# Down projections of two expert groups moved ahead of the expert selection, with gating a group later, one-hot matrices built on VectorE alone, and low weight parts written in place

## The chip, the cores and the metric

The program runs on one NeuronCore of a Trainium2 chip. Its engines are TensorE (PE in the profile, with its weight loads as PEld), VectorE (DVE), ScalarE (ACT), GpSimd (POOL) and SyncE (SP, which here only issues transfers). They run side by side and order themselves by semaphores. The metric is the device time of one execution in microseconds (us), as the median of several runs.

## The reference

Two transformer blocks in float32 are applied to 256 tokens of width 2048. The part that the change rearranges is the mixture of experts at the end of the first block ("peer"): each token has 8 heads, each head picks 16 of 128 x 128 = 16384 experts, and every picked expert is one row of `w_down` and one row of `w_up`.

```python
q = einsum(xn, w_query); s = einsum(q, sub_keys)            # 8 heads, 2 halves, 128 keys
top_s, top_i = lax.top_k(s, 16)
cand = top_s[..., 0, :, None] + top_s[..., 1, None, :]       # 16 x 16 sums
cand_s, cand_i = lax.top_k(cand.reshape(..., 256), 16)
expert = i1 * 128 + i2
gates = softmax(cand_s)
a = gelu(einsum('cd,ced->ce', xc, w_down[expert])) * gates
out = einsum('ce,ced->cd', a, w_up[expert])
```

Around it stand an attention with a pooling branch before, and in the second block a differential and a latent attention with a gated feed-forward layer.

## The kernel before

**Dense experts.** The kernel does not gather rows. It multiplies all 16384 rows of `w_down` with the tokens, applies gelu, multiplies with a gate matrix G (expert x token, zero where the token did not pick the expert), and multiplies the result with all rows of `w_up`. The work is cut into 8 groups of 2048 experts. A group is 32 weight tiles of 1 MB (128 partitions x 2048 columns): 16 down tiles and 16 up tiles. So the stage has 256 tiles.

**Split precision.** A weight tile is used in four pieces of 512 columns. For each piece ScalarE copies the weights to a rounded high part (`high`, the activation in line 518), VectorE subtracts it from the weights to get the low part (`low`, line 1250), and TensorE forms three products for each of the four 128-column blocks of the piece (`piece`, lines 875 to 877): high x high, high x low and low x high. That is 48 matmuls of 256 columns a tile. `w_parts` holds the parts of four pieces, high beside low, so ScalarE and VectorE can be at most one tile ahead.

**The ring.** SyncE loads weight tiles into a ring of 4 slots. A slot is loaded again when VectorE has made the last low part from it (`split=` in `load`, a wait on `lo_ready`).

**Selection and gate matrix.** After the query projection (stage `wq`, 16 tiles) VectorE picks the best 16 of each half (`best`), then for two halves of the tokens (`tb`) the best 16 of the 256 sums, and turns them into indices and gates (lines 1427 to 1456). Then, in 64 steps of 4 tokens, it builds two one-hot matrices: `oh2` (line 1468) and `oh1` (line 1469), each 128 x 4 x 128. GpSimd multiplies `oh2` with the gates (line 490), and TensorE multiplies the two (line 1045), which gives the 128 x 128 gate matrix of one token. ScalarE copies it out and stores it to a scratch tensor in HBM (line 664). While this goes on, no weight tile is multiplied.

**The peer loop.** In each of the 8 turns of the loop VectorE makes the low parts of the next tile, then handles one tile: for a down tile `gated` (lines 1478, 1481, 1482: times G, high part, low part), for an up tile `expert_out` (line 1488: adds to the residual `hT`). The gating of a down tile follows on that tile's own gelu. In every second tile VectorE also reduces one row block of the second block's modulation matrix (`ada`, 12 a turn, lines 1508 and 1511), and 4 of them a second time with another vector (1508, written to PSUM). GpSimd loads these into two buffers, and one transfer of 2 MB a turn brings G of the group.

The order of the work on each engine is written out by hand; every engine runs its own list in order.

Of the kernel before, what the change touches and what calls it, by code (L numbers as in the profile page):

```python
# [13 lines left out]
P = 128  # L14
T = 256
# [34 lines left out]
OHT, OHB = 4, 4  # L50
TWO = 2
# [35 lines left out]
for _name, _n in (("mask0", 3 * P), ("mask1", 3 * T), ("cos1", T), ("sin1", T), ("perm1", P),  # L87
                  ("ident", P), ("cos2", T), ("sin2", T), ("perm2", P), ("iota", P), ("rcount", 4 * T), ("ones", P)):
    CONST[_name] = (_t, _t + _n)
    _t += _n  # L90
# [60 lines left out]
def build_program(nc, A, out):  # L151
    with ExitStack() as ctx:
# [13 lines left out]
        modt = sb("modt", [P, 16])  # L166
# [9 lines left out]
        assert nc.lookup_mloc("cb").addr == arena_at + 121 * 1024  # L176

# [45 lines left out]
        W1 = split_room("w_parts_1", 84, PIECES, 2, PB * P)  # L223

        GH, GL = split_room("merged_high", 0, KC, T), split_room("merged_low", 16, KC, T)
        WO = split_room("w_parts_out", 32, PIECES, 2, PB * P)
# [6 lines left out]
        oh1 = [room(56 + 4 * j, OHT, P) for j in range(OHB)]  # L233
        oh2 = [room(58 + 4 * j, OHT, P) for j in range(OHB)]
        stage = [room(72 + 8 * j, P, BLK) for j in range(2)]
        topv = room(72, 2 * KC, TOPK)
        topi = room(74, 2 * KC, TOPK, dt=U32)
        topf = room(90, KC, TOPK)
        cv = room(91, EH, TOPK)
        ci = room(91.5, EH, TOPK, dt=U32)  # L240
        ca = room(92, EH, TOPK, dt=U32)
        cbi = room(92.5, EH, TOPK, dt=U32)
        caf = room(93, EH, TOPK)
        cbf = room(93.5, EH, TOPK)
        ids = room(94, 3, EH * TOPK)
        idT = room(96, 3, T)
        gsum = room(99, EH)
# [3 lines left out]
        WP = split_room("w_parts", 80, PIECES, 2, PB * P)  # L251
        junk = ps[:, 4:8, :].rearrange("p a b -> p (a b)")
        gl = room(99.5, 2, T)
# [4 lines left out]
        W2 = split_room("w_parts_2", 113, PIECES, 2, PB * P)  # L258
# [19 lines left out]
        WO2 = split_room("w_parts_out_2", 0, PIECES, 2, PB * P)  # L278

        HH, HL = split_room("hidden_high", 32, FF, T), split_room("hidden_low", 92, FF, T)  # L280
        WF = split_room("w_parts_ff", 76, PIECES, 2, PB * P)
# [76 lines left out]
        oh_pool = sem("oh_pool")  # L358
# [5 lines left out]
        at_ready = sem("at_ready")  # L364
        lam_exp = sem("lam_exp")
# [22 lines left out]
        def _(sp):  # L388
            def load(slot, src, made, n=D, split=None):
# [8 lines left out]
            def stream(name, src, count, n=D, o_name=None):  # L398

                o = OUTS[o_name or name]  # L400
                with sp.Fori(0, count // U) as i:
                    for u in range(U):
                        load(u, src[i * U + u], i * U + (o + u + 1 - RING), n)
# [1428 lines left out]
```

## Time and profile before

| | us |
|---|---|
| median of 3 runs | 4149.68 |
| fastest and slowest run | 4144.1, 4150.41 |
| profiled execution, first to last instruction (its span) | 4145.4 |
| PE busy | 3714.2 (90%) |
| PEld busy | 3546.5 (86%) |
| DVE busy | 2687.2 (65%) |
| ACT busy | 1669.0 (40%) |
| POOL busy | 174.1 (4%) |
| mean granted TensorE clock | 0.957 of full speed |

The span is taken inside one profiled execution; the median of the runs is 4.3 us above it, which is what lies around the first and the last instruction. Busy shares are means over stages that differ much: in one stretch of some 220 us before the peer loop TensorE has little to do, and VectorE has almost no idle time. A busy PE is not a PE at its peak, since matmuls are pipelined: in the peer loop one matmul is shown with 0.28 us and they start every 0.12 us.

### The profile page before, as it was taken

The numbers are of one execution on the slowest core, as the hardware profiler recorded it, in microseconds if no ns is written. First come the engines' busy times: TensorE is split into PE (matmuls) and PEld (weight loads), VectorE is DVE, ScalarE is ACT, GpSimd is POOL, SyncE is SP. The second block draws the span as 40 slices with busy tenths as digits, with TensorE's granted clock in tenths as the row PEclk, the third lists the DMA queues.
The fourth block names the chain that finished last, engine by engine and source line by source line (L and its number), as shares of the span: only waits on it lengthen the run. The fifth ranks groups of instructions, "written<-read, shape, count | busy, mean of one in ns | idle before, by whom it ended". The sixth has DMA issues, their size and how long they took to land.

```text
span 4145.4 us, 73928 instructions
## 1 busy us (share of the span) xinstructions
PE 3714.2 (90%) x27694; PEld 3546.5 (86%) x27694; DVE 2687.2 (65%) x4416; ACT 1669.0 (40%) x2865; POOL 174.1 (4%) x240
## 2 busy tenths in 40 slices
PE   0888999891789999999999999979988989999998
PEld 0887888891689999999999999968955989999997
DVE  7865433579967768777777777662237566666554
ACT  0532211440244444444444444442226455555443
POOL 0000000001600000000000000000000000000000
PEclk8999999995899999999999999989999999999999
DMA  9875774440367576766767676622220435555453
GB/s 412 323 263 194 273 288 148 152 163 20 132 244 285 212 287 225 273 240 260 254 255 252 249 282 223 256 92 92 93 80 1 151 134 182 182 182 181 161 178 129
DMA packets 129661, 829.37 MB, mean 200 GB/s; under 512 B 12784, under 2 KB 29296, under 8 KB 38256
## 3 DMA queue, kind: packets, MB, share of 16 engines
q1 hardware_dynamic: 87984, 619.20, 40.7%
q0 software_dynamic: 24768, 189.80, 12.4%
q10 hardware_dynamic: 16640, 16.78, 1.2%
q8 instruction: 168, 2.75, 0.3%
q14 instruction: 101, 0.83, 0.1%
HBM read 806.86 MB, written 18.87 MB: 199 GB/s over the span
## 4 chain that ended last, share of the span: by engine, by line
PE 81%; DVE 10%; issue 4%; DMA 2%; ACT 2%; DVEq 0%; SPq 0%; POOL 0%; ACTq 0%; POOLq 0%
PE ps L875 22%; PE ps L877 21%; PE ps L876 21%; PE ps L851 8%; DMA arena<-in_ada 2%; PE ps L907 1%; PE ps L909 1%; PE ps L910 1%; PE ps L845 1%; DVE arena L1468 1%; DVE w_parts L1250 1%; DVE arena L1469 1%; ACT w_parts L518 1%; PE ps L1152 1%; ACT arena L518 0%
## 5 line engine op out<-in xcount | busy, mean ns | idle before, releaser
L518 ACT ACTIVATE w_parts<-ring 128x512 fp32r<-128x512 f32 x1352 | 851.5, 632 | 1185.9 <-PE ps L877 1042.4
L1250 DVE TENSOR_TENSOR w_parts<-ring,w_parts 128x512 fp32r<-128x512 f32 x1352 | 899.1, 690 | 639.5 <-ACT w_parts L518 617.7
L875 PE MATMUL ps<-x_high,w_parts 128*128 128x256 f32 (+1 forms) x3040 | 892.7, 294 | 135.4 <-DVE w_parts L1250 116.4
L876 PE MATMUL ps<-x_low,w_parts 128*128 128x256 f32 (+1 forms) x3040 | 884.0, 291 | 0.0
L877 PE MATMUL ps<-x_high,w_parts 128*128 128x256 f32 (+1 forms) x3040 | 883.5, 291 | 0.0
L875 PEld LDWEIGHTS ps<-x_high,w_parts 128*128 128x128 f32 x3040 | 587.8, 193 | 155.1 <-DVE w_parts L1250 111.2
L876 PEld LDWEIGHTS ps<-x_low,w_parts 128*128 128x128 f32 x3040 | 588.1, 193 | 6.7
L877 PEld LDWEIGHTS ps<-x_high,w_parts 128*128 128x128 f32 x3040 | 587.7, 193 | 6.9
L875 PE MATMUL ps<-at_high,w_parts 128*128 128x256 f32 x2048 | 580.4, 283 | 0.0
L876 PE MATMUL ps<-at_low,w_parts 128*128 128x256 f32 x2048 | 579.5, 283 | 0.0
L877 PE MATMUL ps<-at_high,w_parts 128*128 128x256 f32 x2048 | 579.5, 283 | 0.0
L1250 DVE TENSOR_TENSOR w_parts_ff<-ring,w_parts_ff 128x512 fp32r<-128x512 f32 (+1 forms) x544 | 363.1, 676 | 245.8 <-ACT w_parts_ff L518 239.2
L518 ACT ACTIVATE w_parts_ff<-ring 128x512 fp32r<-128x512 f32 (+1 forms) x544 | 336.3, 619 | 384.7 <-PE ps L877 384.5
L875 PE MATMUL ps<-x_high,w_parts_ff 128*128 128x256 f32 x1408 | 399.6, 284 | 17.1 <-DVE w_parts_ff L1250 17.1
L876 PE MATMUL ps<-x_low,w_parts_ff 128*128 128x256 f32 x1408 | 399.4, 284 | 0.0
L877 PE MATMUL ps<-x_high,w_parts_ff 128*128 128x256 f32 x1408 | 399.3, 284 | 0.0
L875 PEld LDWEIGHTS ps<-at_high,w_parts 128*128 128x128 f32 x2048 | 393.1, 192 | 0.9
L876 PEld LDWEIGHTS ps<-at_low,w_parts 128*128 128x128 f32 x2048 | 393.2, 192 | 0.0
L877 PEld LDWEIGHTS ps<-at_high,w_parts 128*128 128x128 f32 x2048 | 393.1, 192 | 0.0
L851 PE MATMUL ps<-arena,ring 128*128 128x256 f32 (+1 forms) x1536 | 344.6, 385 | 1.9 <-DVE arena L1226 1.3
L851 PEld LDWEIGHTS ps<-arena,ring 128*128 128x128 f32 x1536 | 290.7, 190 | 49.1 <-issue 8.5
L518 ACT ACTIVATE arena<-ps 128x256 f32<-128x256 f32 (+3 forms) x350 | 154.5, 444 | 412.8 <-PE ps L851 245.7
(212 smaller groups left out, 5899.0 us busy)
## 6 DMA issues: line engine op xcount, KB each, us to landing
ada<-in_ada POOLq DMA_DIRECT2D x160, 1024.0 KB, 5.1
ring<-in_peer_down SPq DMA_DIRECT2D x128, 1024.0 KB, 5.2
ring<-in_peer_up SPq DMA_DIRECT2D x128, 1024.0 KB, 5.0
ring<-in_w_in SPq DMA_DIRECT2D x102, 1024.0 KB, 4.8
ring<-in_w_up SPq DMA_DIRECT2D x88, 1024.0 KB, 4.8
ring<-in_w_down SPq DMA_DIRECT2D x64, 704.0 KB, 4.0
arena<-in_ada SPq DMA_DIRECT2D x32, 1024.0 KB, 19.5
ring<-in_w_out SPq DMA_DIRECT2D x16, 1024.0 KB, 4.8
```

Source lines behind the costliest of these rows:

```text
L518: return nc.scalar.activation(*a, **k)
L845: ins = mm(ps[:, 4, 0:cols], ones, sqd[:, k, :], start=(k == 0), stop=(k == n - 1))
L851: ins = mm(to, ring[:, slot % RING, (at + k) * P:(at + k + 1) * P], moving(k), start=(k == 0), stop=(k == n - 1))
L875: mm(to, w_high, high(k), start=(k == 0), stop=False)
L876: mm(to, w_high, low(k), start=False, stop=False)
L877: ins = mm(to, w_low, high(k), start=False, stop=(k == k_all - 1))
L907: mm(to, high[:, k, tok], w_high, start=(k == 0 and tb % 2 == 0), stop=False, skip_group_check=True)
L909: mm(to, low[:, k, tok], w_high, start=False, stop=False, skip_group_check=True)
L910: ins = mm(to, high[:, k, tok], w_low, start=False, stop=(k == KC - 1), skip_group_check=True)
L1152: ins = mm(ps[:, 7, (u % 2) * P:(u % 2 + 1) * P], vv[:, kb, h * P:(h + 1) * P], wt2[u % 2][:, kb * P:(kb + 1) * P], start=(kb == 0), stop= ...
L1250: vv.tensor_tensor(parts[:, m, 1, 0:w], ring[:, slot, j * PB * P:j * PB * P + w], parts[:, m, 0, 0:w].bitcast(F32), ALU.subtract).then_inc ...
L1468: vv.tensor_tensor(oh2[j], many, idT[:, 1, tok].unsqueeze(2).broadcast_to([P, OHT, P]), ALU.is_equal)
```

## The change

**What moves.** The 32 down tiles of groups 0 and 1 are multiplied before and during the selection and the building of the gate matrix. Their gelu results are kept in two buffers (`held`), which lie in the room of the old `ada` buffers and at the end of the arena. From then on the order of tiles is up(g), down(g + 2), and the gating of group g + 1 runs on VectorE beside the down tiles of group g + 2, from `held`. The PE loop over 8 turns of 32 tiles becomes 32 tiles, a loop of 3 turns of 64 tiles, and 32 tiles. The selection is cut into 12 parts (`choose`), each behind the low parts of one tile.

**One-hots.** The matrices are built on VectorE alone with `tensor_scalar` instructions of 128 x 128: three a token, 12 a step. The first compares with one pointer scalar, the second and the third compare and multiply with the high and the low part of the gate (two pointer scalars). GpSimd's multiplication is gone. TensorE multiplies the rounded type, two matmuls a token. A step stands behind each piece of the tiles 16 to 28, and a fifth behind each tile.

**Low parts in the ring.** VectorE writes the low part over the weights in the ring (`ring_low`), `w_parts` holds high parts alone, and a ring slot is loaded again when TensorE has used the tile (`acc_full`), in the last stage when it has used the pieces.

**Modulation rows.** The 96 row blocks are read in the 3 turns (30 a turn) and the last 32 tiles (6), through one buffer `ada2`. Of three blocks in a row the first is reduced twice: in an odd tile with the context vector, in the next tile with the other, and only then is the buffer free.

VectorE in the loop before, up tiles (line 1488 `expert_out`, line 1511 a modulation row, line 1250 low parts; `ISA` is the reduction, its second row reads the sum):

```order
L1488 SCALAR_TENSOR_TENSOR hT<-ps,mod,hT 128x256
L1511 ISA ada,modt<-ada,cb 128x2048
L1511 ISA modt 128x1
L1249 REGISTER_ALU
L1250 TENSOR_TENSOR w_parts<-ring,w_parts 128x512
L1249 REGISTER_ALU
L1250 TENSOR_TENSOR w_parts<-ring,w_parts 128x512
L1249 REGISTER_ALU
L1250 TENSOR_TENSOR w_parts<-ring,w_parts 128x512
L1249 REGISTER_ALU
L1250 TENSOR_TENSOR w_parts<-ring,w_parts 128x512
L1487 REGISTER_ALU
```

Here one reduction stands behind `expert_out`, and the tile after it has none.

VectorE in the loop now, in the second tile of a turn (line 1620 `expert_out`, 1656 the wait for the load, 1627 the reduction with the context vector):

```order
L1620 SCALAR_TENSOR_TENSOR hT<-ps,mod,hT 128x256
L1656 ISA
L1627 ISA ps,modt<-const,cb 128x2048
L1627 ISA modt 128x1
L137 ISA
```

Four low parts and the next tile's `expert_out` follow. The same list one tile further (1624 the reduction with the other vector, behind which the buffer is free):

```order
L1335 TENSOR_TENSOR ring_low<-ring,w_parts 128x512
L1619 REGISTER_ALU
L1620 SCALAR_TENSOR_TENSOR hT<-ps,mod,hT 128x256
L1624 ISA const,modt<-const,cb 128x2048
L1624 ISA modt 128x1
L1334 REGISTER_ALU
L1335 TENSOR_TENSOR ring_low<-ring,w_parts 128x512
```

Now two of them follow in neighbouring tiles, and a third, which needs a newly loaded buffer, in the tile after.

VectorE behind the selection before (line 1456 the last of the gates, 1468 and 1469 the one-hots of one step):

```order
L1455 RECIPROCAL arena<-arena 128x8
L1456 TENSOR_TENSOR arena<-arena 128x128
L1462 UNCONDITIONAL_BRANCH
L1462 ISA
L1468 ISA
L1468 TENSOR_TENSOR arena<-const,arena 128x512
L1469 ISA
L1469 TENSOR_TENSOR arena<-const,arena 128x512
L1466 REGISTER_ALU
```

VectorE at that place now (line 1580 the last of the gates, 1631 the low part of the gates, 1602 to 1604 the three one-hots of one token; three more tokens of the step follow before the next row of line 1335):

```order
L1579 RECIPROCAL const<-const 128x8
L1580 TENSOR_TENSOR const<-const 128x128
L1335 TENSOR_TENSOR ring_low<-ring,w_parts 128x512 x4
L1631 TENSOR_TENSOR const<-const 128x256
L1602 TENSOR_SCALAR one_hots<-const 128x128
L1603 TENSOR_SCALAR one_hots<-const 128x128
L1604 TENSOR_SCALAR one_hots<-const 128x128
L1602 TENSOR_SCALAR one_hots<-const 128x128
```

Two instructions a step became twelve, and low parts of weight tiles stand between the steps.

TensorE there now (lines 919 to 921 the three products of a down tile, 1095 and 1096 the high and low gates of a token):

```order
L920 MATMUL ps<-x_low,w_parts 128x256
L921 MATMUL ps<-x_high,ring_low 128x256
L1095 MATMUL ps<-one_hots 128x128
L1096 MATMUL ps<-one_hots 128x128
L1095 MATMUL ps<-one_hots 128x128
L1096 MATMUL ps<-one_hots 128x128
L1095 MATMUL ps<-one_hots 128x128
L1096 MATMUL ps<-one_hots 128x128
L1095 MATMUL ps<-one_hots 128x128
L1096 MATMUL ps<-one_hots 128x128
L919 MATMUL ps<-x_high,w_parts 128x256
```

Before, only the gate matmuls stood there, four a step. The core of the diff:

```diff
+        ring_low = nc.alloc_sbuf_tensor_at("ring_low", [P, RING, D], F32R, offset=nc.lookup_mloc("ring").addr)[:]
-        WP = split_room("w_parts", 80, PIECES, 2, PB * P)
+        WP = split_room("w_parts", 80, PIECES, PB * P)
+        hots = split_room("one_hots", 32, OHB, 3, OHT, P)
+        ada2 = spare(0, D)
+        held = [ada[:, :, :].rearrange("p a b -> p (a b)").rearrange("p (a b) -> p a b", a=16), room(88, 16, T)]
...
@@ SyncE @@
-                if split is not None:
-                    sp.wait_ge(lo_ready, split)
...
-                        load(t, src[t], None, split=16 + SPLIT[name] + PIECES * (t + 1 - RING))
+                        load(t, src[t], OUTS[name] + t + 1 - RING)
...
@@ GpSimd @@
-                    nc.gpsimd.tensor_tensor(
-                        oh2[j], oh2[j], idT[:, 2, tok].unsqueeze(2).broadcast_to([P, OHT, P]), ALU.mult,
-                    ).then_inc(oh_pool, 1)
...
+            gates_in(0, 0, 0)
+            gates_in(0, 0, 1)
+            with pool_e.Fori(0, 3) as i:
+                for r in range(ADA_ALL):
+                    pool_e.wait_ge(a2_free, i * ADA_ALL + (r + 1))
+                    pool_e.dma_start(ada2, A["ada"][i * ADA_ALL + (97 + r)]).then_inc(a2_in, 16)
+                    if r in (14, 29):
+                        gates_in(i, 32, 2 + r // 15)
...
@@ TensorE @@
-                    w_high, w_low = (parts[:, m, h, b * P:(b + 1) * P] for h in range(2))
+                    w_high = parts[:, m, b * P:(b + 1) * P]
+                    w_low = ring_low[:, slot, (at + b) * P:(at + b + 1) * P]
...
+            for s in range(32):
...
+                for j in range(PIECES):
+                    peer_piece(0, 0, s, s, j, XH, XL)
+                    if s == 16 and j == 0:
+                        pe.wait_ge(ids_copied, 2)
+                    if s >= 16 and 5 * (s - 16) + j < STEPS:
+                        gates_of(5 * (s - 16) + j)
...
+                if s in (10, 15):
+                    turn_ids((s - 10) // 5)
...
@@ VectorE @@
+            def hot_step(n):
+                dve.wait_ge(g_full, n + 1)
+                for q in range(OHT):
+                    t = OHT * n + q
+                    one_hot = hots[:, n % OHB, :, q, :]
+                    id1, id2 = idT[:, 0, t:t + 1], idT[:, 1, t:t + 1]
+                    vv.tensor_scalar(one_hot[:, 0, :], iota, id1, None, ALU.is_equal)
+                    vv.tensor_scalar(one_hot[:, 1, :], iota, id2, gate_h[:, t:t + 1], ALU.is_equal, ALU.mult)
+                    ins = vv.tensor_scalar(one_hot[:, 2, :], iota, id2, gate_l[:, t:t + 1], ALU.is_equal, ALU.mult)
+                ins.then_inc(oh_dve, 1)
...
+            for s in range(16):
+                peer_low(0, 0, s)
+                if s < 4:
+                    heads_best(12 + s)
+                else:
+                    choose((s - 4) // 6, (s - 4) % 6)
...
+            for s in range(16, 31):
+                for j in range(PIECES):
+                    if 5 * (s - 16) + j < STEPS:
+                        hot_step(5 * (s - 16) + j)
+                    low_piece(WP, SPLIT["peer"] + PIECES * (s + 1) + 1, s + 1, (s + 1) % RING, j)
+                if 5 * (s - 16) + 4 < STEPS:
+                    hot_step(5 * (s - 16) + 4)
+            for u in range(16):
+                gated(0, 0, 0, u, ATH, ATL)
+                if u % 4 == 3:
+                    low_piece(WP, SPLIT["peer"] + PIECES * 32 + 1, 32, 0, u // 4)
...
+            with dve.Fori(0, 3) as i:
+                for v in range(64):
+                    peer_low(i, 64, 33 + v)
+                    if v % 32 < 16:
+                        expert_out(i, 64, v % 16, 32 + v)
+                    else:
+                        gated(i, 32, 1 + v // 32, v % 16, ATH, ATL)
+                    r = (v - 1) // 2
+                    if v % 2 and r < ADA_ALL:
+                        dve.wait_ge(a2_in, i * (16 * ADA_ALL) + 16 * (r + 1))
+                        if r % 3 == 0:
+                            ada_ctx(modt[:, 30 + r // 3:31 + r // 3])
+                        else:
+                            ada_x(modt[:, ADA_X + r - r // 3 - 1:ADA_X + r - r // 3])
+                    if v % 2 == 0 and v and r % 3 == 0 and r < ADA_ALL:
+                        ada_x(modt[:, r // 3:r // 3 + 1])
```

## Rows read from the trace of the kernel before

**Rows 1.** The page's first line.

```profile
span 4145.4 us, 73928 instructions
```

**Rows 2.** Stretches: length, PE, PEld, DVE, ACT, POOL busy, PEclk, DMA share, GB/s.

```profile
932.00:1010.00 78.00, 1.80 (x6) 1.00 (x6) 74.47 (x206) 3.38 (x6) 0.00 (x0) 0.51 0.00 0
1010.00:1120.00 110.00, 78.05 (x424) 66.82 (x424) 110.00 (x110) 31.16 (x53) 69.50 (x54) 0.82 0.34 116
```

**Rows 3.** Timeline of ScalarE: start, length, instruction, idle before and its releaser.

```profile
930.27 0.38 ACT L518 ACTIVATE arena<-ps 128x256 f32<-128x256 f32 x1 [5.15 <-PE ps L877]
```

**Rows 4.** Timeline of TensorE in the peer loop.

```profile
1156.23 0.58 PE L875 MATMUL ps<-x_high,w_parts 128*128 128x256 f32 x1 [14.13 <-DVE w_parts L1250]
...
1349.83 0.58 PE L875 MATMUL ps<-x_high,w_parts 128*128 128x256 f32 x1 [2.92 <-issue]
...
1411.66 0.39 PE L875 MATMUL ps<-x_high,w_parts 128*128 128x256 f32 x1 [0.26 <-DVE w_parts L1250]
...
1541.93 0.38 PE L875 MATMUL ps<-x_high,w_parts 128*128 128x256 f32 x1 [2.56 <-DVE hT L1488]
```

**Rows 5.** The chain of waits: start, length, what, between 800 and 980.

```profile
822.52 6.42 DVE x_low L1264 x16
...
940.24 2.21 DVE cb L1430
...
974.03 2.21 DVE cb L1430
```

**Rows 6.** Timeline of VectorE around the selection's end.

```profile
957.83 0.23 DVE L1433 TENSOR_SCALAR arena<-arena 128x128 uint32<-128x128 uint32 x1
957.98 0.22 DVE L1434 TENSOR_SCALAR arena<-arena 128x128 uint32<-128x128 uint32 x1
...
1007.20 0.29 DVE L1456 TENSOR_TENSOR arena<-arena 128x128 f32<-128x128 f32 x1
1009.40 0.69 DVE L1468 TENSOR_TENSOR arena<-const,arena 128x512 f32<-128x512 f32 x1 [1.91 <-ACT arena L518]
```

**Rows 7.** Groups of VectorE, 750 to 1130: count, busy us, mean ns, idle before.

```profile
L1469 DVE TENSOR_TENSOR arena<-const,arena 128x512 f32<-128x512 f32 x60 | 90.5, 1509 | 0.0
...
L1264 DVE SCALAR_TENSOR_TENSOR x_low<-arena,mod,x_high 128x256 fp32r<-128x256 f32 x16 | 6.4, 480 | 0.0
```

**Rows 8.** Groups of VectorE, whole span: two pointer scalars, then one.

```profile
L1576 DVE TENSOR_SCALAR ada<-ada,small 128x512 f32<-128x512 f32 x16 | 8.7, 546 | 0.6
L1582 DVE TENSOR_SCALAR ada<-ada,small 128x512 f32<-128x512 f32 x16 | 7.8, 486 | 0.6
```

**Rows 9.** Timeline of VectorE in the peer loop: a down tile, then an up tile.

```profile
1395.27 0.42 DVE L1478 TENSOR_TENSOR arena<-arena 128x256 f32<-128x256 f32 x1
...
1396.66 2.29 DVE L1511 CUSTOM_DVE_ANT_0 ada<-ada,cb 128x2048 f32<-128x2048 f32 x1 [0.19 <-DVE at_low L1482]
...
1454.68 2.29 DVE L1511 CUSTOM_DVE_ANT_0 ada<-ada,cb 128x2048 f32<-128x2048 f32 x1
...
1456.88 1.90 DVE L1250 TENSOR_TENSOR w_parts<-ring,w_parts 128x512 fp32r<-128x512 f32 x3
1459.43 0.69 DVE L1250 TENSOR_TENSOR w_parts<-ring,w_parts 128x512 fp32r<-128x512 f32 x1 [0.66 <-ACT w_parts L518]
```

**Rows 10.** Timeline of GpSimd beside those up tiles.

```profile
1457.62 0.53 POOL L476 DMA_DIRECT2D ada<-in_ada  x1 [10.14 <-DVE modt L1511]
1469.14 0.53 POOL L476 DMA_DIRECT2D ada<-in_ada  x1 [10.99 <-DVE modt L1511]
```

**Rows 11.** Timeline of GpSimd: a load of 1 MB is issued.

```profile
397.12 0.53 POOL L476 DMA_DIRECT2D ada<-in_ada  x1 [8.16 <-DVE mod L1210]
```

**Rows 12.** Timeline of VectorE: the reduction that waited for that load.

```profile
402.21 2.29 DVE L1210 CUSTOM_DVE_ANT_0 ada<-ada,cb 128x2048 f32<-128x2048 f32 x1 [3.53 <-DMA ada<-in_ada]
```

**Rows 13.** Transfers issued from 1130 to 1160: count, KB, median us to landing.

```profile
gates_scratch<-arena ACTq DMA_DIRECT2D x2, 1024.0 KB, 7.6
arena<-gates_scratch POOLq DMA_DIRECT2D x1, 2048.0 KB, 8.2
```

More of the change, by code:

```diff
@@ L388, in _, with load @@
         def _(sp):
-            def load(slot, src, made, n=D, split=None):
+            def load(slot, src, made, n=D):
                 if made is not None:
                     sp.wait_ge(acc_full, made)
-                if split is not None:
-                    sp.wait_ge(lo_ready, split)
                 sp.dma_start(ring[:, slot % RING, 0:n], src).then_inc(w_slot[slot % RING], 16)
[L398 to L403, printed above, removed]
             sp.dma_start(cb[:, 0, :], A["c"]).then_inc(c_in, 16)
@@ L656, in _ @@
[L656 to L665 removed]
+                cols = slice(tb * P, (tb + 1) * P)
@@ L867, in tokens_first, with piece @@
                 return ins
-            def piece(to, parts, m, wait, first, n, high, low, k_all):
+            def piece(to, parts, m, wait, slot, at, first, n, high, low, k_all):
                 pe.wait_ge(lo_ready, wait)
@@ L1028, in _, with peer_piece, turn_ids @@
                     keys_of(n // 2 - 1)
-            keys_of(EH - 1)
-            for tb in range(2):
+            def peer_piece(i, per, at, u, j, high, low):
+                ins = piece(ps[:, u % BANKS, 0:T], WP, j, i * (per * PIECES) + (16 + SPLIT["peer"] + PIECES * at + j + 1),
+                            u % RING, PB * j, PB * j, PB, lambda k: high[:, k, :], lambda k: low[:, k, :], KC)
+                ins.then_inc(piece_used if j < PIECES - 1 else acc_full, 1)
+            def turn_ids(tb):
                 pe.wait_ge(ids_ready, tb + 1)
@@ new lines, in up_tile @@
+            def up_tile(i, per, g, u, at, high, low):
+                if u < BANKS and g < 7:
+                    pe.wait_ge(gelu_done, i * (per // 2) + (16 * (g + 2) - BANKS + u + 1) if g < 6 else 125 + u)
+                else:
+                    pe.wait_ge(up_free, i * (per // 2) + (16 * g + u - BANKS + 1))
+                for j in range(PIECES):
+                    if u == 0:
+                        pe.wait_ge(at_ready, i * (per // 2) + (16 * g + PB * (j + 1)))
+                    peer_piece(i, per, at, u, j, high, low)
@@ new lines, in _ @@
+            ch.leave(3)
+            dve.wait_ge(acc_full, OUTS["peer"] + 224)
+            for v in range(32):
+                if v < 31:
+                    peer_low(0, 0, 225 + v)
+                expert_out(0, 0, v % 16, 224 + v)
+                if v < 16:
+                    gated(0, 0, 7, v, XH, XL)
+                r = v // 2 - 8
+                if v % 2 and 0 <= r < 6:
+                    dve.wait_ge(a2_in, 16 * (3 * ADA_ALL + r + 1))
+                    if r % 3 == 0:
+                        ada_ctx(modc[:, 30 + r // 3:31 + r // 3])
+                        ada_x(mod2[:, 30 + r // 3:31 + r // 3])
+                    else:
+                        ada_x(mod2[:, 92 + r - r // 3 - 1:93 + r - r // 3 - 1])
```

494 lines of the change are left out of this document (276 added, 218 removed).

## The prediction, made before the change was run

> **What bounds the kernel now.** I read the stretches first, to see which engine fills each stage, then the chain of waits, then the timelines of the engines in turn. The profiled execution spans 4145.4 us [rows 1]; the median of the runs is 4149.7, so 4.3 us are added at the end. Two places matter.
>
> The first is the selection. The last tile of the query projection is copied out at 930.27 [rows 3], so TensorE ends it at 930.1, and the first tile of the peer loop starts at 1156.23 [rows 4]. Between them VectorE works without a break: 74.5 of 78 us in the selection and 110 of 110 while the one-hots are built [rows 2]. VectorE is the bound for 226 us, with TensorE all but idle in the first part.
>
> The second is the peer loop. GpSimd's loads follow VectorE's reductions in every second tile, 11.52 us apart [rows 10], so an undisturbed tile takes 5.76 us: TensorE is the bound there. A turn of 32 tiles takes 1541.93 - 1349.83 = 192.1 us [rows 4] where 32 x 5.76 is 184.3. The other 7.8 us are the branch back (2.9 [rows 4], "issue") and small waits for low parts such as the 0.26 of [rows 4].
>
> **The change part by part.** I follow the engines from 930.1 until tile 32 (the first up tile) is done. Before, tile 32 is the first of the second turn, done at 1349.8 + 5.9 = 1355.7.
>
> *Four tiles under the last of the first selection.* They run at TensorE's pace: 4 x 5.76 = 23.0, and 0.9 for the last key products (an estimate for a few short float32 matmuls): 954.0. The low parts of tile 4 are ready 1.5 us later: the fourth one of a tile starts 0.8 behind the tile boundary, after ScalarE's copy, and takes 0.69 [rows 9]. So the 12 parts of the selection begin at 955.5.
>
> *Selection with low parts between.* One round of the selection takes 974.03 - 940.24 = 33.8 us [rows 5], two take 67.6. Between the 12 parts stand 11 tiles' low parts. A row of three takes 1.90 [rows 9], so one starts each 0.60 and four take 2.5 us: 27.5. VectorE needs on the mean 2.5 + 5.6 = 8.1 us a tile and TensorE 5.76, so VectorE sets the time: 955.5 + 67.6 + 27.5 = 1050.6.
>
> *Hand-over.* From the last gate to the first one-hot 1.9 us pass [rows 6], for the transposes and a copy. A second copy, four low parts beside them and the gates' low part are added: I take 3.1: 1053.7.
>
> *One-hots.* The trace has no 128-column `tensor_scalar` with a pointer, so its price is bounded. Below: two without a pointer start 0.15 apart [rows 6], another pair 0.14; 0.145 x 12 = 1.74 us a step. A second pointer makes the 512-column one longer by 546 - 486 = 60 ns [rows 8]. Whether a queue hides that: the 16 instructions of line 1264, with one pointer, take 480 ns each [rows 7] and 6.42 together [rows 5], so they start each 0.40, 0.08 less than their length; low parts, without a pointer, start 0.09 before the end of the one in front. The overlap is the same, so a pointer counts in full. A token has 1 + 2 + 2 = 5 pointers: a step is 4 x (3 x 0.145 + 5 x 0.06) = 2.9 us. Above: no overlap at all, 4 x (3 x 0.225 + 5 x 0.06) = 3.9. I take 2.9, to which the rows with pointers are nearest. 64 steps are 186 us and 52 low parts 31: 217.
>
> Is VectorE the bound there? The next low part needs TensorE's piece (1.44), ScalarE's copy with signals (0.75) and the gate products in front (0.65, estimated as eight short matmuls at 0.08), 3.0 in all behind the step before; VectorE is at it after 0.6 + 2.9 = 3.5. So yes, at full clock. At half clock the same chain takes about 5.1, and a step with a low part 4.4 in place of 3.5. The granted clock was 0.82 of full speed in the one-hot stage before [rows 2], where TensorE was also kept waiting. If the clock is half for a quarter of the stretch, 52 pieces lose about 0.2 each: 10 us, and I take 4 more for the selection and for the restart behind it. So the last step ends at 1053.7 + 217 = 1270.7.
>
> *What is late next.* Gating of group 0 needs G from HBM. After the last step come the last copy and store (1.6 to its issue; landing 7.6 when two loads ran beside it [rows 13], I take 6), GpSimd's start (0.65: the reduction at 1454.68 and its read end at 1456.97, the load starts at 1457.62 [rows 9, 10]) and the 2 MB load, 8.2 [rows 13]: 16.5. Then 16 gatings of 1.2 us (1395.27 to the reduction at 1396.66, less its wait [rows 9]), with four low parts between, 22, and the last piece, 2.2: 41. Tile 31 was done after 17, so TensorE waits most of 18 us. Tile 32 is done at 1270.7 + 41 + 14 = 1325.7. Gain so far: 1355.7 - 1325.7 = 30.
>
> *The loop of 64 tiles.* Gating from `held` waits for no gelu, and the branch comes back 3 times, not 7: both are small gains, counted below. What is added is a wait. A modulation buffer that is reduced twice is freed in an even tile, and the very next tile needs the new load. In an up tile: reduction at 1454.68, load issued at 1457.62 [rows 9, 10], in the buffer 402.21 - 397.12 = 5.09 later [rows 11, 12]: 1462.7. VectorE is at that reduction at 1454.68 + 5.76 = 1460.4 and stands 2.3 us. Queued behind it are the low parts of the next tile: they start at 1462.7 + 2.2 = 1464.9. To keep TensorE fed they must start by 1463.6: the fourth low part at 1459.43 follows the tile boundary by 0.8 (ScalarE's copy), so the boundary is at 1458.6, one tile later 1464.4, less 0.75 for the low part. TensorE waits 1.3 us. In a down tile VectorE gets to the reduction 0.9 later (gating takes 1.2, `expert_out` 0.4), so 2.2, and 0.2 of small waits as before. A turn of 64 tiles has ten such places, 4 beside down and 6 beside up tiles: 9.6 + 7.8. With the branch 2.9, 3 for the two loads a turn that run beside G's 8.2 us [rows 13] (an estimate) and 0.7 for the rest: 24. So three turns take 3 x (368.6 + 24) = 1178, the last 32 tiles 184.3 + 4 = 188: 1366. Before, 7 x 192.1 = 1345. Loss: 21.
>
> *The ring.* A slot is now free one tile later. From there to ScalarE's first use of the new tile it is 2.25 tiles, 13 us, against 5.1 for a load of 1 MB [rows 11, 12]. I cost it at nothing in every stage. Without that cover each tile that waits costs its own lateness; 1 us on each of the 64 last tiles (8 us of cover in place of 13) would be the first to show. The POOL multiplication that goes is off the path once VectorE is the bound, but it had kept line 1469 at 1509 ns [rows 7] where line 1468, of the same shape, takes 690 [rows 6]. That is why twelve instructions for two cost so little more: 2.9 against 2.1 a step.
>
> **The sum.** 4145.4 - 30 + 21 = 4136.4, and 4.3 around it: 4141.
>
> Two rules of the Trainium skill bear on the step. "VectorE: DVE Perf Modes", section "The TRN2 errata", has 58 cycles plus half the columns for such an instruction, 0.127 us at 0.96 GHz by its figures, 1.5 us a step as an estimate from the page; the rows give 0.145 without a pointer, and the page has nothing for pointers. By it the first rival would be right. The same page, section "The DRAIN you can't avoid", says that an instruction does not start before the pipe in front is empty. By it the third rival would be right; the trace disagrees, 0.15 us between starts of instructions of 0.23 [rows 6].
>
> **The rivals.**
> *Pointers are free in a row of instructions.* A step is 1.74. Then not VectorE but the chain through TensorE and ScalarE limits two steps: (3.8 + 1.74) / 2 = 2.8 with a low part, 13 us a tile, 166 for the stage instead of 217. 51 less: 4090. For it: pairs at 0.145. Against it: line 1264.
> *The load's wait is covered.* If the loads land a tile earlier than I reckon, or the low parts have more slack, 3 x 17 = 51 us of the loop's loss go: 4090. Against it: the 5.09 us is measured with one transfer alone and could hardly be less. This is also the case in which the loop simply does as before.
> *Steps without overlap (the other side).* Each one-hot starts when the one in front has ended: 3.9 a step, 64 us more: 4205. It decides from 3.1 us a step on, where the gain of 30 is down to 17 and the whole is no faster.
> *The clock stays at half through the one-hots.* 52 pieces x 0.9 = 47, less the 10 I have: 4178. For it: TensorE would work 2.1 of 3.5 us. Against it: busy all the time at half clock, it should get the full one back, as in the stage before, which had 0.82.
>
> **How the numbers follow.** Forecast 0.42 (its own range 4112 to 4170), free pointers 0.20, covered wait 0.08, no overlap 0.14, half clock 0.10, something else 0.06. The range 4075 to 4203 leaves out the ends of the first and third rival. 0.2% is 8.3 us, about what a measurement of this kernel can tell from no change: faster is below 4141.4. The forecast lies on that edge: about half of its cases are faster, four tenths the same, the rest slower. With the rivals: faster 0.50, same 0.18, slower 0.32.
>
> **What would show it.** Right: the group of one-hots at 0.28 and 0.34 us a piece, starts 0.2 to 0.27 apart, 16 to 17 us a tile in tiles 16 to 28; tile 32 spread over some 18 us behind the G load; in the loop DVE waiting about 2.3 us for `ada2` ten times a turn, PE 1.3 or 2.2 us behind it; a turn of 64 tiles of 392 us. Wrong: a step under 2.4 or over 3.4 us; a turn under 380; ScalarE waiting for ring loads anywhere.

## The result and the profile after

The changed kernel takes 4191.3 us (median of 4 runs, 4185.3 to 4197.0), the kernel before 4146.9 in the same comparison. The ratio is 1.0104 with a 95% interval of 1.0090 to 1.0118: slower by 1%, where 4141 and no loss was forecast. The profiled execution took 4190.2.

The page's first line of the kernel after [before: rows 1]:

```profile
span 4188.6 us, 73007 instructions
```

I cut both executions at the first matmul of tile 33 (tile 32 is then done) and at the first split matmul of the second block, and did the same with two kernels of the experiments. TensorE in the kernel before at both cuts, then in the kernel after: the start of tile 32, the first cut, the starts of the second and third turn of 64 tiles and of the last 32 tiles, and the second cut [before: rows 4]:

```profile
1357.03 0.28 PE L875 MATMUL ps<-x_high,w_parts 128*128 128x256 f32 x1
2742.75 0.58 PE L875 MATMUL ps<-x_high,w_parts 128*128 128x256 f32 x1 [16.34 <-DVE w_parts L1250]
```

```profile
1315.92 0.58 PE L919 MATMUL ps<-at_high,w_parts 128*128 128x256 f32 x1 [10.64 <-DVE ring_low L1335]
1333.88 0.41 PE L919 MATMUL ps<-at_high,w_parts 128*128 128x256 f32 x1
1738.18 0.38 PE L919 MATMUL ps<-at_high,w_parts 128*128 128x256 f32 x1 [1.91 <-DVE ring_low L1335]
2147.48 0.38 PE L919 MATMUL ps<-at_high,w_parts 128*128 128x256 f32 x1 [1.97 <-DVE ring_low L1335]
2554.57 0.28 PE L919 MATMUL ps<-at_high,w_parts 128*128 128x256 f32 x1
2802.94 0.58 PE L919 MATMUL ps<-x_high,w_parts 128*128 128x256 f32 x1 [16.34 <-DVE ring_low L1335]
```

| us | before | ring's part alone | after | both repairs |
|---|---|---|---|---|
| start until tile 32 is done | 1357.0 | 1345.3 | 1333.9 | 1299.2 |
| tile 33 to the second block's first split matmul | 1385.7 | 1361.9 | 1469.1 | 1363.1 |
| the rest | 1402.7 | 1388.0 | 1385.7 | 1385.7 |
| span | 4145.4 | 4095.2 | 4188.6 | 4047.9 |

Up to tile 32 the kernel after gains 23, in the stages behind the mixture of experts 17, and the peer loop loses 83. Turns of 64 tiles take 422.3 (tile 32's 18 us in it), 409.3 and 407.1, against the 392.6 forecast.

VectorE's longest waits in the loop, 1340 to 2740 (total, times, longest):

```profile
DVE ring_low L1335 <- ACT w_parts L531: 241.6, 364, 3.9
DVE const L1624 <- DMA const<-in_ada: 110.5, 31, 6.7
DVE arena L1613 <- DMA arena<-gates_scratch: 5.9, 1, 5.9
```

The first row costs nothing: VectorE has caught up with TensorE and waits for the next copy, in the kernel before as well. The second is new, and it is the forecast wait for `ada2`, but at 3.6 us on the mean, not 2.3. I call such a wait and the two tiles that it touches a place. Beside an up tile it is what was forecast. GpSimd issues the load at 1797.20, VectorE has it 5.05 later:

```profile
1797.20 0.53 POOL L515 DMA_DIRECT2D const<-in_ada  x1 [16.43 <-DVE modt L1624]
```
```profile
1799.52 0.48 DVE L1620 SCALAR_TENSOR_TENSOR hT<-ps,mod,hT 128x256 f32<-128x256 f32 x1
1802.25 2.29 DVE L1624 CUSTOM_DVE_ANT_0 const<-const,cb 128x2048 f32<-128x2048 f32 x1 [2.25 <-DMA const<-in_ada]
```

Beside a down tile it is not. GpSimd, then SyncE, then the two transfers (median us to landing), then VectorE:

```profile
1869.63 0.53 POOL L515 DMA_DIRECT2D const<-in_ada  x1 [16.90 <-DVE modt L1624]
```
```profile
1869.88 0.33 SPq L412 DMA_DIRECT2D ring<-in_peer_down  x1
```
```profile
const<-in_ada POOLq DMA_DIRECT2D x1, 1024.0 KB, 7.4
ring<-in_peer_down SPq DMA_DIRECT2D x1, 1024.0 KB, 7.4
```
```profile
1877.10 2.29 DVE L1624 CUSTOM_DVE_ANT_0 const<-const,cb 128x2048 f32<-128x2048 f32 x1 [4.69 <-DMA const<-in_ada]
```

The last reader frees the modulation buffer at the tile boundary, and since the change TensorE frees the ring slot at that boundary too. Both loads start within 0.25 us and each takes 7.4. Beside the up tile a ring load ran too, but it was issued 1.19 us behind the modulation load, and there the later one alone is late (6.3). The rate of all transfers is the same in both cases (length, PE busy, PEclk, DMA share, GB/s):

```profile
1798.39 0.33 SPq L412 DMA_DIRECT2D ring<-in_peer_up  x1
```
```profile
ring<-in_peer_up SPq DMA_DIRECT2D x1, 1024.0 KB, 6.3
```
```profile
1799.50:1803.50 4.00, 4.00 (x37) 1.00 1.01 426
1871.80:1875.80 4.00, 3.66 (x32) 1.00 1.01 426
```

So 2 MB are in after some 7.5 us either way, and what counts is whether the modulation load has a start. In the three turns, 12 places beside up tiles have one of 1.18 to 1.52 us, and its load lands after 5.0 to 5.3; the 12 beside down tiles have at most 0.37, and it lands after 6.9 to 8.8.

Then TensorE stands, and comes back at its lower clock:

```profile
1875.18 0.28 PE L921 MATMUL ps<-x_high,ring_low 128*128 128x256 f32 x1
1880.06 0.58 PE L919 MATMUL ps<-x_high,w_parts 128*128 128x256 f32 x1 [4.60 <-DVE ring_low L1335]
1880.44 0.41 PE L920 MATMUL ps<-x_low,w_parts 128*128 128x256 f32 x1
1880.65 0.41 PE L921 MATMUL ps<-x_high,ring_low 128*128 128x256 f32 x1
...
1884.06 0.38 PE L919 MATMUL ps<-x_high,w_parts 128*128 128x256 f32 x1
1884.28 0.29 PE L920 MATMUL ps<-x_low,w_parts 128*128 128x256 f32 x1
1884.40 0.29 PE L921 MATMUL ps<-x_high,ring_low 128*128 128x256 f32 x1
```

Starts are 0.21 apart until 1884, 0.12 from there. The granted clock in between (same columns):

```profile
1880.40:1883.90 3.50, 3.50 (x18) 0.50 0.67 241
```

From first matmul to first matmul the tile in which it waits takes 10.5 us, the next one 7.7, where 5.65 is undisturbed.

VectorE while the one-hots are built, first a wait, then one token's three and the next token's first two:

```profile
1122.71 0.69 DVE L1335 TENSOR_TENSOR ring_low<-ring,w_parts 128x512 fp32r<-128x512 f32 x1 [2.62 <-ACT w_parts L531]
1123.32 0.28 DVE L1602 TENSOR_SCALAR one_hots<-const 128x128 fp32r<-128x128 f32 x1
1123.52 0.34 DVE L1603 TENSOR_SCALAR one_hots<-const 128x128 fp32r<-128x128 f32 x1
1123.77 0.34 DVE L1604 TENSOR_SCALAR one_hots<-const 128x128 fp32r<-128x128 f32 x1
1124.03 0.28 DVE L1602 TENSOR_SCALAR one_hots<-const 128x128 fp32r<-128x128 f32 x1
1124.22 0.34 DVE L1603 TENSOR_SCALAR one_hots<-const 128x128 fp32r<-128x128 f32 x1
```

A token takes 0.71, so a step 2.83: the forecast 2.9 held. But a tile takes 19.2 us (median), where VectorE has work for 5 x 2.83 + 4 x 0.61 = 16.6.

### The profile page after: what moved, and what is told of

Its sections match the earlier page's. It is cut to its first block, busy times and chain, and to the rows that moved or that the text cites. A ratio compares the mean times of both kernels' runs of the same rounds, so it can differ in the third digit from the quotient of the medians.

```text
span 4188.6 us, 73007 instructions
## 1 busy us (share of the span) xinstructions
PE 3703.8 (88%) x27694; PEld 3536.9 (84%) x27694; DVE 2720.1 (65%) x5042; ACT 1670.5 (40%) x2863; POOL 91.5 (2%) x176
## 4 chain that ended last, share of the span: by engine, by line
PE 72%; DVE 14%; DMA 8%; issue 4%; ACT 2%; DVEq 0%; SPq 0%; POOLq 0%; ACTq 0%
PE ps L919 19%; PE ps L920 19%; PE ps L921 18%; PE ps L894 8%; DMA const<-in_ada 5%; DVE ring_low L1335 3%; DMA arena<-in_ada 2%; PE ps L953 1%; PE ps L956 1%; PE ps L955 1%; DVE one_hots L1604 1%; DVE one_hots L1603 1%; PE ps L888 1%; DVE one_hots L1602 1%; ACT w_parts L531 1%
## 5 line engine op out<-in xcount | busy, mean ns | idle before, releaser
L921 PE MATMUL ps<-x_high,ring_low 128*128 128x256 f32 (+1 forms) x4704 | 1359.0, 289 | 0.0
L1335 DVE TENSOR_TENSOR ring_low<-ring,w_parts 128x512 fp32r<-128x512 f32 x1352 | 894.7, 690 | 562.1 <-ACT w_parts L531 549.0
L919 PE MATMUL ps<-x_high,w_parts 128*128 128x256 f32 (+1 forms) x3296 | 975.7, 296 | 171.9 <-DVE ring_low L1335 171.8
L921 PEld LDWEIGHTS ps<-x_high,ring_low 128*128 128x128 f32 x4704 | 914.2, 194 | 7.0
L919 PEld LDWEIGHTS ps<-x_high,w_parts 128*128 128x128 f32 x3296 | 646.2, 196 | 189.7 <-DVE ring_low L1335 140.0
L919 PE MATMUL ps<-at_high,w_parts 128*128 128x256 f32 x1792 | 510.4, 285 | 59.1 <-DVE ring_low L1335 59.1
L1335 DVE TENSOR_TENSOR ring_low<-ring,w_parts_ff 128x512 fp32r<-128x512 f32 (+1 forms) x544 | 361.4, 676 | 233.1 <-ACT w_parts_ff L531 228.4
L921 PE MATMUL ps<-at_high,ring_low 128*128 128x256 f32 x1792 | 507.6, 283 | 0.0
L919 PE MATMUL ps<-x_high,w_parts_ff 128*128 128x256 f32 x1408 | 392.6, 279 | 17.1 <-DVE ring_low L1335 17.1
L919 PEld LDWEIGHTS ps<-at_high,w_parts 128*128 128x128 f32 x1792 | 342.4, 191 | 64.4 <-DVE ring_low L1335 60.2
```

Of the source, the lines that this page charges most:

```text
L919: mm(to, w_high, high(k), start=(k == 0), stop=False)
L921: ins = mm(to, w_low, high(k), start=False, stop=(k == k_all - 1))
L1335: vv.tensor_tensor(ring_low[:, slot, cols], ring[:, slot, cols], parts[:, m, 0:w].bitcast(F32), ALU.subtract).then_inc(lo_ready, 1)
```

## The experiments

Each is compared with the kernel before on the same chip. My two theories after the result were: the loop's loss is the wait for the single modulation buffer, and the one-hot stage is lengthened by a chain through TensorE and ScalarE. A third question was why stages that only the ring's edit touches are faster.

### The ring's part alone

```diff
-                    w_high, w_low = (parts[:, m, h, b * P:(b + 1) * P] for h in range(2))
+                    w_high = parts[:, m, b * P:(b + 1) * P]
+                    w_low = ring_low[:, slot, (at + b) * P:(at + b + 1) * P]
...
-                    load(u, src[i * 16 + u % 16], None,
-                         split=i * (32 * PIECES) + (16 + SPLIT["peer"] + PIECES * (u + 1 - RING)))
+                    load(u, src[i * 16 + u % 16], i * 32 + (first + u))
```

> The kernel before with one part of the change alone: low parts written over the weights in the ring, w_parts with high parts alone, and a ring slot loaded again when TensorE has used the tile. Selection, one-hots, gating and the two modulation buffers stay as they were. Theory (address): in the profile after, the split matmuls start 0.1178 us apart on the mean (0.117, 0.118, 0.118) where before they start 0.120 apart, in every stage, whatever else the change moved; so this part brings 48 x 0.0022 = 0.106 us a tile, 406 tiles: 43 us, and the time is 4147 - 43 = 4104, with an undisturbed tile of 5.654. Rival (nothing): the closer starts come from the new order of the work or from the time at which ring loads run, and this part alone is what I costed it at, nothing: 4147. Rival (cover): ring loads that start a tile later are missed somewhere: ScalarE waits for them and the time is over 4147.

Measured: 4103.5 us, ratio 0.9899 (0.9882 to 0.9915). The stretch 3420 to 3600 lies in the last layer, TensorE busy without a gap at full clock. First the kernel before, then this one (columns as in rows 2):

```profile
3420.00:3600.00 180.00, 180.00 (x1503) 180.00 (x1502) 120.51 (x219) 98.53 (x165) 0.00 (x0) 1.00 0.51 181
```
```profile
3420.00:3600.00 180.00, 180.00 (x1530) 180.00 (x1529) 122.16 (x223) 99.19 (x167) 0.00 (x0) 1.00 0.52 184
```

1530 matmuls stand where 1503 did: on the mean they start 0.1178 us apart in place of 0.1200. The expectation miscounted the tiles; there are 24480 such matmuls, 54 us at most by 2.2 ns each, and 43 were gained, so that its 43 came out is luck. The ring's part, costed at nothing, is a gain of 1%, and the rest of the change costs 4191.3 - 4103.5 = 88, not the 44 by which the whole is slower.

This edit also lets ring loads start at other times. That is not what brings the matmuls closer: in the last weight tiles, where no load runs any more, the distances are the same (the kernel before, then this one; columns length, PE busy, PEclk, DMA share, GB/s), and so they are at a DMA share of 0.9, from 222 to 262.

```profile
4108.00:4116.00 8.00, 8.00 (x69) 1.00 0.00 0
```
```profile
4060.00:4068.00 8.00, 8.00 (x70) 1.00 0.00 1
```

And it is not the matmul that reads the low part alone: from 3420 to 3600 each of the three products starts closer to the next, 0.1175, 0.1175 and 0.1183, where each had 0.1200.

### High and low parts in buffers apart

```diff
-        WP = split_room("w_parts", 80, PIECES, 2, PB * P)
+        WP = split_room("w_parts", 80, 2, PIECES, PB * P)
```

> The kernel before with w_parts laid out as all high parts, then all low parts (2 x 4 x 512), where high and low of one piece lay side by side (4 x 2 x 512). Same instructions, same ring. Theory A (neighbours): the 0.120 us between matmuls come from high and low lying within one 4 KB piece; with the two apart it is 0.1178 as in the kernel after, 43 us less: 4104. Theory B (ring): what counts is that low comes out of the ring and not out of the buffer that ScalarE writes; here it stays 0.120 and the time 4147.

Measured: 4148.0 us, ratio 1.0004 (0.9994 to 1.0013), and the same stretch:

```profile
3420.00:3600.00 180.00, 180.00 (x1503) 180.00 (x1502) 121.07 (x220) 98.27 (x165) 0.00 (x0) 1.00 0.51 181
```

The neighbours in the buffer are not the reason. What is left is that the low part lies in the ring's room. Whether its address, or that ScalarE writes the other buffer, matters was not tried: the cause stays open.

### Ring loads out of the modulation load's way

```diff
+                    if v in (25, 31, 55, 61):
+                        sp.wait_ge(piece_used, i * 192 + (PIECES - 1 + USED["peer"] + 3 * (v + 29) + 3))
+                        load(v, src, None)
+                    else:
                         load(v, src, i * 64 + (first + 32 + v))
```

> The kernel after; in a turn of 64 tiles four ring loads (those that are released in the same instant as the modulation load of the four places beside down tiles) wait until TensorE has used three pieces more, about 4.2 us longer. Theory (collision): the modulation load issued at 1869.63 and the ring load at 1869.88 took 7.4 us each, where a load alone takes 5.05; VectorE stood 4.7 us, TensorE 4.9, and then it ran 35 matmuls at half clock, 2.0 more. With the ring load out of the way the modulation load lands after 5.05 to 5.3, TensorE stands some 2.5 at these places and its clock stays up: 12 places x (6.9 - 2.5) = 53 less: 4191 - 53 = 4138. Rival (latency): the load is late in these places for another reason (its place in GpSimd's queue, the reduction that frees the buffer), the landing stays at 7 and the time at 4190. Rival (clock at any gap): the wait falls to 2.5, but the clock falls to half after it as before: 12 x 2.4 = 29 less, 4162.

Measured: 4159.8 us, ratio 1.0023 (1.0012 to 1.0033); ten runs spread from 4144 to 4172. GpSimd, SyncE, VectorE and TensorE at the same place as above:

```profile
1870.07 0.53 POOL L520 DMA_DIRECT2D const<-in_ada  x1 [16.90 <-DVE modt L1629]
```
```profile
1874.66 0.33 SPq L412 DMA_DIRECT2D ring<-in_peer_down  x1
```
```profile
1875.11 2.29 DVE L1629 CUSTOM_DVE_ANT_0 const<-const,cb 128x2048 f32<-128x2048 f32 x1 [2.27 <-DMA const<-in_ada]
```
```profile
1878.07 0.39 PE L924 MATMUL ps<-x_high,w_parts 128*128 128x256 f32 x1 [2.18 <-DVE ring_low L1340]
```

The load takes 5.04 in place of 7.4: the collision is shown. Of the clock neither expectation held in full, and the time is next to the 4162 of the rival in which the clock falls at any gap. Of the 12 places beside down tiles, 8 still have a next tile of 7.2 to 8.6 us, 4 have 5.8; a place costs 3.8 on the mean in place of 7.0. That is 38 less in 12 places; the medians are 31.5 apart, the two profiled executions 18.5 (the one here is the slowest of the ten). The places beside G's load became longer in the profiled run (12.4, 12.0 and 9.7 us for the tile, before 11.6, 8.7 and 8.3).

### The buffer free a tile earlier

The second reduction reads `cb` in place of the buffer and takes the same 2.29 us, so ten modulation values a turn are others and the kernel's result is not the reference's.

```diff
                             ada_ctx(modt[:, 30 + r // 3:31 + r // 3])
+                            dve.sem_inc(a2_free, 1)
...
-                        ada_x(modt[:, r // 3:r // 3 + 1])
+                        vv.tensor_tensor_reduce(junk, cb[:, 1, :], cb[:, 0, :], 1.0, 0.0, ALU.mult, ALU.add,
+                                                modt[:, r // 3:r // 3 + 1])
```

> The kernel after; in the three turns of 64 tiles the second reduction of a doubly used row reads the silu rows of cb instead of the modulation buffer (so ten values a turn of the modulation are others), and the buffer is free a tile earlier, behind the reduction with the context vector. VectorE's instructions, their number and order stay. Theory (single buffer): what a turn of 64 loses is VectorE's wait for the load right behind the double use. A turn takes 408 where 64 x 5.654 = 362; ten places make 43 of the 46. With 9 us between free and need the waits go, except beside G (about 3 us a turn): 3 x 40 = 120 less, 4071. Rival (crowding): TensorE waits because two reductions in neighbouring tiles delay the low parts, whatever the load does; then only the collisions go, and the time stays over 4130.

Measured: 4076.5 us, ratio 0.9830 (0.9813 to 0.9846), 115 less than the kernel after. The second and third turn take 371.9 and 370.5, and the up and down places 5.7 to 6.0 a tile; what stays is the one beside G (8.2 or 8.3, and 7.3) and a smaller loss around the start of a turn (7.4 or 7.8, then 6.3 or 7.3). Two reductions in neighbouring tiles are not the cost. The wait is.

### Modulation rows spread over seven tiles

All of the computation is kept.

```diff
-                    r = (v - 1) // 2
-                    if v % 2 and r < ADA_ALL:
+                    k, at = v // 7, v % 7
+                    if k < ADA_X and at in (0, 3, 5):
...
-                    if r in (14, 29):
-                        gates_in(i, 32, 2 + r // 15)
+                    if r in (13, 26):
+                        gates_in(i, 32, 2 + r // 14)
```

> The kernel after, all of its computation kept, with the modulation rows spread so that the one buffer always has two tiles between its last reader and its next: three rows in seven tiles (context vector in tile 0, the other vector in tile 1, the next rows in tiles 3 and 5) where it was three in six; 27 rows a turn of 64 tiles and 15 in the last 32, where both reductions of a row stand in one tile. G's load stands behind the modulation load in GpSimd's queue. Theory (single buffer): the waits of the ten places go as they did with the early freed buffer, a turn takes 371 to 373 where it took 408; the five double reductions in the last 32 tiles cost some 1.5 us each, 5 more than before for three more of them: 4191 - 3 x 37 + 5 = 4085. Rival (GpSimd's queue): G's 2 MB load, or the modulation load behind it, is still waited for twice a turn, 4 us each: 4105.

Measured: 4087.6 us, ratio 0.9852 (0.9837 to 0.9868). The turns take 370.5 and 367.4 after the first. One buffer is enough when each load has two tiles. Of the 8.6 and 5.5 us above 64 undisturbed tiles (361.9), most is lost around the start of a turn: TensorE stands 4.0 there, which the profile puts down to "issue", and the next tile takes 7.3 or 8.2. Why it stands longer there than in the kernel after (1.9) is open. In the last 32 tiles a tile with both reductions costs 1.6 to 2.8 more, and for some of them the next tile 1.4 to 1.6 as well: more than the 1.5 expected.

### Gate products a step later

```diff
-                    if s >= 16 and 5 * (s - 16) + j < STEPS:
-                        gates_of(5 * (s - 16) + j)
+                    if s >= 16 and 0 <= 5 * (s - 16) + j - 1 < STEPS:
+                        gates_of(5 * (s - 16) + j - 1)
```

> The kernel after; while the one-hots are built, TensorE's gate products of a step (and ScalarE's copy of them) stand one piece later: piece j, then the gates of step n - 1 in place of n. Same instructions. The stage takes 19.2 us a tile where VectorE's own work is 5 x 2.83 + 4 x 0.61 = 16.6. Theory (chain): VectorE waits, 29.5 us in 1055 to 1287, since a low part needs ScalarE's copy, that needs the piece, and that stands behind gate products which need the step just built; with a step more of slack the chain no longer binds, TensorE is idle less and its clock rises: 17 us a tile, 12.8 x 2.2 = 28 less: 4163. Rival (half clock binds): the waits come in the stretches at half clock, where a piece and eight gate products are 20 x 0.213 = 4.3 us of TensorE for 3.44 of VectorE, whatever stands first; the order changes little: under 8 us, 4183 to 4191.

Measured: 4158.9 us, ratio 1.0029 (1.0019 to 1.0039), 32 less than the kernel after. The stretch 1060 to 1240, after and then this one:

```profile
sum 180.00, PE 129.08 PEld 122.44 DVE 155.28 ACT 54.50 POOL 0.00; mean PE 129.08 PEld 122.44 DVE 155.28 ACT 54.50 POOL 0.00
```
```profile
sum 180.00, PE 142.29 PEld 137.13 DVE 180.00 ACT 63.79 POOL 0.00; mean PE 142.29 PEld 137.13 DVE 180.00 ACT 63.79 POOL 0.00
```

VectorE has no idle time left, a tile takes 16.2 to 17.4, on the mean 16.6, and the last one-hot ends at 1254.7 in place of 1287.1. The mean granted clock of this stretch is 0.84 in both kernels, so the rival (half clock binds) is out: the chain was the cause.

### One-hots without the gate's low part

The kernel after without the third one-hot of a token and its matmul, so the gates are rounded.

> The kernel after without the third one-hot of a token (the low part of the gate) and without its matmul: the gates are rounded. Theory (VectorE bounds the stage, a pointer counts in full): a step is 4 x (0.195 + 0.255) = 1.8 us where it was 2.83, a tile 5 x 1.8 + 2.4 = 11.4 plus the waits, some 13.5; 12.8 tiles x 5.7 = 73 less, 4118. Rival (TensorE's and ScalarE's chain bounds it): the low parts still come every 3.8 us or so as now, less four short products (0.45): 12.8 x 5 x 0.45 = 29 less, 4162.

Measured: 4133.5 us, ratio 0.9959 (0.9949 to 0.9969), 58 less than after, where one theory gave 73 and the other 29. A tile of the stage takes 14.8 (median), VectorE's work is 11.4. Its waits, 1055 to 1285:

```profile
DVE ring_low L1334 <- ACT w_parts L531: 47.5, 43, 2.8
```

So both theories hold in part. A tile became 4.4 us shorter where 5.2 of VectorE's work and some 2.2 of the chain (the expectation's 0.45 a step) went, and VectorE now waits 43 times: below 14.8 us a tile the chain, as it is ordered here, holds it up.

### Both repairs together

> Both edits, the spread modulation rows and the gate products a step later, all of the computation kept. If the two are independent the gains add: 4191 - 106 for the rows, and 28 for the gates by the chain theory (4057) or under 8 by the half-clock theory (4077 to 4085). Either is below the 4103.5 of the ring's part alone, and then the whole change, without its single-buffer wait, is worth 20 to 45 us more than its ring alone.

Measured: 4049.5 us (4046.3 to 4056.4, 5 runs), ratio 0.9764 (0.9751 to 0.9777). All of the computation is kept; it beats both kernels. VectorE's waits for modulation rows, 1305 to 2600:

```profile
DVE ps L1627 <- DMA const<-in_ada: 3.9, 4, 1.2
DVE const L1624 <- DMA const<-in_ada: 3.1, 4, 1.1
```

The gains add: 104 and 32 apart, 142 together. Against the ring's part alone, everything else in the change (the moved down projections, the one-hots, the single buffer) is then worth 54 us by the medians and 47 in the two profiled executions, of which the table has 46 up to tile 32.

## Why the prediction was wrong

**The step that failed** is the price of the added wait, 1.3 us beside an up tile and 2.2 + 0.2 beside a down tile: "4 beside down and 6 beside up tiles: 9.6 + 7.8". In the kernel after, a place beside a down tile costs 7.0 us and not 2.4 (12 places: 84, forecast 29), one beside an up tile 2.0 and not 1.3 (15 places: 30, forecast 20; the first of a turn costs 3.2, its load lands after 6.6; the others 1.7), the three beside G 5.9 each (18, forecast 13). That is 70 of the 86 us by which the loop was missed (the sum below). Some 12 more are the kernel with the ring's part alone, which waits less between turns than the kernel before; the other 4 were not followed up. The mechanism, its ten places a turn and VectorE's wait of 2.3 beside up tiles were right. The size was wrong twice. I took 5.09 for the landing, from rows 11 and 12, as that of a load alone; it was not alone, a ring load was issued 1.08 us behind it, so it had such a start. And I counted the ring's edit apart, though it moves the ring loads to the tile boundary, where the buffer also comes free, and takes the start away beside down tiles. A ring load starts 1.85 us behind a tile's last matmul in the kernel before and 0.31 in the kernel with the ring's part alone (medians in the loop). In the latter, 28 modulation loads are issued within 0.2 us of a ring load and land after 7.3 to 8.9; its two buffers hide that. And I let TensorE come back at full clock after each gap; after 4.9 us it ran at 1.2 GHz for 4 us, and the next tile took 2.0 more. The forecast had a term for the clock in the one-hot stage, none in the loop.

**The ring, costed at nothing,** brought 43 us. The cover of 13 us held, as forecast: ScalarE waits for no ring load in any of the kernels. I had looked at the loads alone; no row of the kernel before could show the closer starts.

**Selection.** From 920.0 TensorE needs 7.1 to 9.0 a tile in tiles 4 to 15, 8.1 forecast, and the first one-hot starts at 1042.0. The forecast 1053.7 started from 930.1; 10.1 of the 11.7 us between the two are those that the earlier stages gained.

**The step of the one-hots** was right: 0.28 and 0.34 us a piece, 0.20 and 0.25 apart, 2.83 for 2.9. That pointers are free in a row, and that nothing overlaps, both fell. The second pointer was not priced by itself, though: in rows 8, as in the one-hots, the instruction with two pointers also does two operations and the other does one, so the 60 ns may belong to either. **Their stage** was not: 1287.1 - 1042.0 = 245 us for 217 + 10. The working compared the chain, 3.0 at full clock (its terms, 1.44 + 0.75 + 0.65, add up to 2.84) and 5.1 at half, with VectorE's 3.5 and 4.4, and took half clock for a quarter of the time at 0.2 a piece. The granted clock was 0.84, so half clock for about a third, and the waits did not go with it: with one step of slack they are gone at the same clock. The kernel after has few and long waits of VectorE in 1055 to 1287:

```profile
DVE ring_low L1335 <- ACT w_parts L531: 29.5, 14, 2.6
```

With the gate products a step later the stage takes 212.

**Behind the last one-hot** 41 us were forecast, and 1333.9 - 1287.1 = 46.8 passed. GpSimd issues G's load 12.6 after it (8.3 forecast), and VectorE has G 11.0 after that, not 8.2:

```profile
1299.66 0.53 POOL L502 DMA_DIRECT2D arena<-gates_scratch  x1 [11.73 <-DMA gates_scratch<-arena]
```
```profile
1310.69 0.42 DVE L1613 TENSOR_TENSOR ada<-ada,arena 128x256 f32<-128x256 f32 x1 [9.66 <-DMA arena<-gates_scratch]
```

**The sum in the two profiles.** Against the kernel with the ring's part alone, the rest gains 11.4 up to tile 32 (30 forecast) and loses 107 behind it (21 forecast). The errors are 19 and 86, less the 50 of the ring between these two executions: 55 above the 4136.4 forecast for the profiled execution. With 2 us that the rest of the table gains, 4189.

**The rule** of the Trainium skill, "VectorE: DVE Perf Modes", section "The TRN2 errata", gives 0.127 us for each of these instructions as an estimate, and nothing for pointers. The measured 0.20 and 0.25 disagree with it, and decide. Its section "The DRAIN you can't avoid" has the next instruction wait for an empty pipe, and adds that one which is not held starts earlier. The trace agrees with the addition, which the prediction left out: the next starts 0.09 us before the end of the one in front.

## What to carry to other kernels

When a change shares out fewer buffers, price the wait with every transfer that the same event releases, and ask how long TensorE stands: here two loads met at the tile boundary and the clock fell behind the gap, and 2.4 us became 7. Before buying a buffer, see whether the load that is waited for can be issued ahead of the others (here 1.2 us were enough), or give it two tiles between its last reader and its next. Where two engines hand work to each other every few microseconds, try one step of slack in the order: here it added no instruction and took out all of VectorE's waits in the stage. Run the parts of a change apart: the part thought free was the gain that hid half of the loss.

## What was not expected of the hardware

- The same matmuls start 0.1178 us apart when the low part of the weights is read from the ring's room, and 0.1200 when it is read from `w_parts`, all three products and whether or not loads run. Why is open.
- TensorE's clock after a gap: after 4.9 us it came back at 1.2 GHz; after gaps of some 2.4 us (one of 3.9), in the kernel with later ring loads, it did so in 8 places of 12. In the kernel after, gaps of 3.2 and 3.3 beside up tiles left it at full clock. So the length of the last gap alone does not tell it.
- Two loads of 1 MB issued 0.25 us apart on two queues took 7.4 us each. With 1.2 us between them the first took 5.0, as with 4.6 us, and only the second was late, 6.3. In the kernel after, the first modulation load that is waited for in each turn is the exception, 6.6 with 1.2 us between; why is open.
- `tensor_scalar` of 128 columns: 0.23 us long and 0.15 apart without a pointer scalar (on integers), 0.28 and 0.20 with one, 0.34 and 0.25 with two and a second operation.
